# Gate columns of four tokens written interleaved into a PSUM bank, and copied out in runs of four

## The reference, cut to what matters

```python
def peer_tokens(xt, w_q, sub_keys, u_experts, v_experts):
    ...
    top_s, j = lax.top_k(cand, PEER_TOPK)
    e = (jnp.take_along_axis(i1, j // PEER_TOPK, axis=-1) * N_KEYS
         + jnp.take_along_axis(i2, j % PEER_TOPK, axis=-1))
    gate = jax.nn.softmax(top_s, axis=-1).astype(xt.dtype)
    u = jnp.take(u_experts, e, axis=0)
    v = jnp.take(v_experts, e, axis=0)
    act = jax.nn.gelu(jnp.einsum('td,thkd->thk', xt, u), approximate=False)
    return jnp.einsum('thk,thkd->td', gate * act, v)
```

## Time and profile before

| what | value |
|---|---|
| median of 3 runs | 1476.38 us (1474.99 to 1478.65) |
| span of the profiled execution | 1475.5 us, the one time that was recorded for it |
| TensorE busy, instructions | 98%, 8568 matmuls |
| VectorE, ScalarE, GpSimd busy | 84%, 43%, 60% |

### The profile page before, as it was taken

One profiled execution on the slowest core, in us unless ns is written; L12 is line 12 of the kernel. 1 busy time (PEld: TensorE's weight loads), 2 busy tenths in 40 slices (PEclk: granted clock), 3 DMA queues, 4 the chain that ended last, 5 costly groups with the idle time before them and its releaser, 6 DMA issues.

```text
span 1475.5 us, 24979 instructions
## 1 busy us (share of the span) xinstructions
PE 1448.1 (98%) x8568; PEld 1323.0 (90%) x8568; DVE 1240.7 (84%) x2516; ACT 628.3 (43%) x846; POOL 885.5 (60%) x552
## 2 busy tenths in 40 slices
PE   6998989999999999999999999999999999999998
PEld 6998989999999999999999999888888888888886
DVE  7999883799999999687888762799999999999985
ACT  6334544333333333366666653433333333333333
POOL 4687533648588888766667666355545555555510
PEclk9999999999999999999999999999999999999999
DMA  5222212748699999879999999999999999999972
GB/s 179 101 72 71 90 58 88 255 144 305 192 334 336 334 331 337 292 268 367 368 353 377 362 367 406 379 373 378 383 403 379 404 382 396 377 407 376 386 248 92
DMA packets 120259, 433.35 MB, mean 294 GB/s; under 512 B 12384, under 2 KB 12640, under 8 KB 118528
## 3 DMA queue, kind: packets, MB, share of 16 engines
q1 hardware_dynamic: 62592, 212.88, 40.0%
q0 software_dynamic: 46080, 167.79, 30.1%
q10 hardware_dynamic: 11520, 51.93, 8.8%
HBM read 379.34 MB, written 52.69 MB: 293 GB/s over the span
## 4 chain that ended last, share of the span: by engine, by line
PE 83%; DVE 1%; issue 0%; ACT 0%; DVEq 0%; ACTq 0%
PE ps_unit L848 36%; PE ps_misc L917 24%; PE ps_unit L917 12%; PE ps_unit L821 6%; PE ps_misc L883 3%; PE ps_misc L786 1%; PE ps_misc L790 0%; PE ps_unit L773 0%; PE ps_misc L913 0%; DVE gate_parts L1599 0%; DVE gate L1552 0%; PE ps_unit L913 0%; PE ps_misc L804 0%; PE ps_misc L902 0%; PE ps_misc L865 0%
## 5 line engine op out<-in xcount | busy, mean ns | idle before, releaser
L514 POOL TENSOR_TENSOR w_lo<-raw,w_hi 128x1024 fp32r<-128x1024 f32 x172 | 417.3, 2428 | 210.5 <-issue 127.6
L578 POOL DMA_INDIRECT rows<-v_rows,expert x160 | 258.8, 1617 | 234.7 <-DVE sums L1464 162.7
L963 ACT ACTIVATE w_hi<-raw 128x1024 fp32r<-128x1024 f32 x300 | 315.4, 1052 | 43.0 <-ACT act_ring L1138 33.7
L1454 DVE CUSTOM_DVE_ANT_0 rows<-rows,ps_unit 128x1024 f32<-128x1024 f32 x160 | 190.8, 1215 | 30.8 <-DMA rows<-u_rows,expert 30.5
L1182 ACT ACTIVATE prod_hi<-prod 128x384 fp32r<-128x384 f32 x128 | 67.3, 526 | 343.1 <-PE ps_unit L917 337.5
L848 PE MATMUL ps_unit<-mov_hi,w_hi 128*128 128x384 f32 x1024 | 205.3, 342 | 0.0
L848 PE MATMUL ps_unit<-mov_hi,w_lo 128*128 128x384 f32 x1024 | 199.9, 337 | 0.0
L848 PE MATMUL ps_unit<-mov_lo,w_hi 128*128 128x384 f32 x1024 | 199.8, 337 | 0.0
L848 PEld LDWEIGHTS ps_unit<-mov_lo,w_hi 128*128 128x128 f32 x1024 | 181.0, 188 | 0.0
L848 PEld LDWEIGHTS ps_unit<-mov_hi,w_lo 128*128 128x128 f32 x1024 | 180.9, 188 | 0.0
L848 PEld LDWEIGHTS ps_unit<-mov_hi,w_hi 128*128 128x128 f32 x1024 | 178.6, 189 | 0.2 <-issue 0.2
(11 more groups left out here) (257 smaller groups left out, 2570.1 us busy)
## 6 DMA issues: line engine op xcount, KB each, us to landing
raw<-stream SPq DMA_DIRECT2D x300, 512.0 KB, 6.0
acts_dram<-act_ring ACTq DMA_DIRECT2D x64, 384.0 KB, 6.4
gates_dram<-gates ACTq DMA_DIRECT2D x12, 2048.0 KB, 10.6
acts_in<-acts_dram SPq DMA_DIRECT2D x32, 768.0 KB, 8.3
gates_even<-gates_dram SPq DMA_DIRECT2D x12, 1024.0 KB, 13.2
gates_odd<-gates_dram SPq DMA_DIRECT2D x12, 1024.0 KB, 12.8
rows<-u_rows,expert POOLq DMA_INDIRECT x160, 7.0
rows<-v_rows,expert POOLq DMA_INDIRECT x160, 8.3
```

The costliest lines, as they stand in the source:

```text
L514: nc.gpsimd.tensor_tensor(w_lo[:, j, :], raw[:, j, :], w_hi[:, j, :].bitcast(F32), ALU.subtract).then_inc(lo_made, 1)
L578: nc.gpsimd.indirect_dma_start(out=rows[:, n % ROWS_RING, :], out_offset=None, in_=table, in_offset=bass.IndirectOffsetOnAxis(ap=expert[:, ...
L963: nc.scalar.activation(w_hi[:, j, :], raw[:, j, :], ACT.Copy).then_inc(hi_made, 1)
L1454: nc.vector.tensor_tensor_reduce(out=rows[:, n % ROWS_RING, :], in0=rows[:, n % ROWS_RING, :], in1=x_rows, scale=1.0, scalar=0.0, op0=ALU. ...
```

## The change

TensorE's output for token x is no longer 128 neighbouring columns but every fourth column of the bank, starting at x. ScalarE reads the bank with the four tokens of a key as neighbours and writes runs of four neighbouring fp32 (16 bytes), one run every 128 bytes. Operands, counts, waits, banks and the layout of `gates` are the same.

```diff
--- before.py
+++ after.py
@@ -880,7 +880,8 @@
                     pe.wait_ge(g_took, n - 1)
                 for x in range(BATCH):
                     for m, g in enumerate((gated_hi, gated_lo)):
-                        last = nc.tensor.matmul(ps_misc[:, b % 2, x * P:(x + 1) * P], hot_j[:, b % 2, x // 2, :, x % 2],
+                        last = nc.tensor.matmul(ps_misc[:, b % 2].rearrange("p (i t) -> p t i", t=BATCH)[:, x, :],
+                                                hot_j[:, b % 2, x // 2, :, x % 2],
                                                 g[:, b % 2, x // 2, :, x % 2], start=(m == 0), stop=(m == 1))
                 last.then_inc(g_done, 1)
 
@@ -1155,8 +1156,8 @@
                 u_unit(U_BEFORE - 1, j)
             def take_gates(tg, s, b):
                 act.wait_ge(g_done, BATCHES * tg + b + 1)
-                nc.scalar.activation(gates[:, s, :, BATCH * b:BATCH * (b + 1)].rearrange("p i t -> p t i"),
-                                     ps_misc[:, b % 2, :].rearrange("p (t i) -> p t i", t=BATCH),
+                nc.scalar.activation(gates[:, s, :, BATCH * b:BATCH * (b + 1)],
+                                     ps_misc[:, b % 2, :].rearrange("p (i t) -> p i t", t=BATCH),
                                      ACT.Copy, scale=1.0 / GATE_UP).then_inc(g_took, 1)
 
             def gate_group(tg):
```

## The result

The changed kernel takes 1512.12 us (median of 4 runs, 1510.94 to 1513.29), before it was 1476.01 us (median of 4, 1474.99 to 1478.65): a ratio of 1.0244 with a 95% interval of 1.0232 to 1.0256, 36.1 us slower. The forecast was 1515.6, with a likeliest range of 1506 to 1523.

What follows compares the result with a forecast made beforehand. TensorE was taken to bound the kernel. Span 1475.5 + 39.2 for scattered matmuls - 0 for shorter copies = 1514.7 us, plus 0.9 from span to median: 1515.6; likeliest range 1506 to 1523, 8 in 10 1473 to 1523.

Steps and rivals of the forecast that it cites:

- The bound: Gate groups, 626 to 872 us: TensorE busy 245.95 of 246.00 us, every other engine waits for it.
- The copy: ScalarE's 96 gate copies, line 1158: from 1167 to 650-750 ns each, saving up to 52.8 us, worth nothing at the end.
- The start of the value stage: After the gates: their last transfer starts about a microsecond earlier, but six microseconds of slack make that worth nothing.
- The price of a scattered matmul: TensorE's gate matmuls, line 883: from 57 to 108 ns each, by ScalarE's copy ratio 1167 / 617 = 1.89.
- A: Gate matmuls: PSUM takes scattered results as fast as neighbouring ones, still 57 ns, 1476 us; chance 0.30.
- B: Gate matmuls: each element pays ScalarE's full 1.07 ns, 106 us more, 1582 us; chance 0.06 with all else above the range.
- C: Gate matmuls: only each pair's accumulating one slows, 19.6 us, 1496 us; chance 0.05 with other prices between no change and forecast.
- The sum: TensorE's path in the gate groups: 768 gate matmuls at 51 ns more each, 39.2 us added, span 1514.7 us.
- D, faster: Gate groups: shorter ScalarE copies release something on the path, some 5 us through the value stage's start, 1471 us; chance 0.03.

Runs made afterwards that it cites:

- the step of 12 bytes: Kernel before, with three tokens' columns interleaved 12 bytes apart, the fourth token in one run, ScalarE copying in two instructions: 1503.39 us, against 1472.37.
- the first experiment: Kernel before with only ScalarE's copy changed to write runs of four, TensorE writing its columns as before: 1476.72 us against 1476.22, ratio 1.0004.
- TensorE's half alone: Kernel before with only the gate matmuls' output interleaved, ScalarE still writing single elements 128 bytes apart: 1513.15 us against 1476.22, ratio 1.0246.

## Why the prediction was right, point by point

**The bound.** That TensorE sets the beat and nobody else is on the path held: it stayed busy for 282.50 of 282.50 us, and the one half of the change that helps ScalarE moved nothing when run alone (ratio 1.0004).

**The copy.** The range of 617 to 1167 ns, with 650 to 750 as the choice, was too high, even at its lower bound: 590 ns. The row taken for that bound, line 1146, is a single copy of its form, and why it took longer stays open; the copies of line 1091, in the same trace, took 595 on average for the same 512 elements:

```profile
L1091 ACT ACTIVATE scores<-ps_misc 128x512 f32<-128x512 f32 x8 | 4.8, 595 | 0.0
L1091 ACT ACTIVATE scores<-ps_misc 128x256 f32<-128x256 f32 x8 | 3.1, 391 | 0.0
```

Nothing on ScalarE's side of the sum hung on it, but the price of the matmul did: by 595 the ratio is 1.96 in place of 1.89, a matmul 112 ns and the sum 42 us.

**The start of the value stage.** As forecast nothing came of the earlier transfer: VectorE's first product waits 15.84 us for the gates in the changed kernel (16.24 in the earlier trace rows), and the stage from the run of 240 matmuls on is 590.2 us (590.1).

**The price of a scattered matmul.** Taken as 108 ns by the ratio of two rows of ScalarE, measured as 109; the rivals A (57) and B (195) fall, and C (a slow second matmul only) with them, since the two of a token start at equal distances. What the runs show is an 8-byte place: pairs at even columns cost 57 ns, pairs at odd ones 109, steps of 8, 12 and 16 bytes 109 or 110. The Trainium skill's page "Advanced Engine Details and Errata", section "Memory Cachelines", gives PSUM lines of 8 bytes, two fp32 values. These figures agree with it. The same section says that any non-contiguous pattern slows matmuls significantly. The runs do not bear that out so widely: the pairs are not contiguous and cost nothing (ratio 0.9997). The ratio of ScalarE's rows gave the right number for a reason that the runs only half bear out. The prediction said that neighbours share an access and scattered elements don't; that fits what TensorE's matmuls cost. But its 1.89 is a property of ScalarE's writes to SBUF, with a fixed part in both durations. By an estimate from the two rows of line 1091, 391 ns for 256 elements and 595 for 512, that part is some 187 ns, and without it the ratio is 2.3 to 2.4. That the 1.89 came so near TensorE's 1.91 was luck.

**The sum.** 768 x 51 = 39.2 us was forecast, and the stretch lost 37.2. The term was too large by its count, not by its price: not all 16 matmuls of a beat pay the surcharge in the beat. The 14 distances from the second gate matmul to the sixteenth grow by 52 ns each, 0.73 us; the first distance grows only from 0.07 (703.74 to 703.81) to 0.09 us (702.04 to 702.13), and the one from the last gate matmul to the U unit from 0.02 to 0.06. The row of before that starts this beat is

```profile
703.74 0.23 PE L883 MATMUL ps_misc<-gated_hi,hot_j 128*128 128x128 f16 x1
```

That makes 0.79 in place of 16 x 51 = 0.82 us, against 0.78 in the chain. With a run at the end of each batch the whole surcharge shows (the step of 12 bytes), so what is missing here is lost where the U unit follows; how the U unit takes it up stays open. Of the 3.3 us by which the forecast span (1514.7) exceeds the measured one, 2.0 are this term. The other 1.3 are the earlier start of the gates, told above, less the 0.1 us behind the stretch, and belong to no part of the change.

**The rivals on the other side.** "D, faster" had 0.03 and fell with the first experiment. A, no change, had 0.30: it was the right thing to fear, because the kernel's trace had no row on it, and it turns out to describe the same edit with even pairs in place of single columns.

## What to carry to other kernels

Before an engine is relieved of a scattered write, look at who has slack: here the copy had 65 us of waiting behind it and the matmul none, so the same scatter was free on one side and cost 37 us on the other. If TensorE must interleave results in a PSUM bank, do it in pairs of fp32 columns that begin at an even one; that kept its pace here, single columns halved it at every step tried (8, 12 and 16 bytes). This is shown for fp16 matmuls of 128 columns alone. Here the reader of PSUM makes it needless: ScalarE read the bank at a step of 512 bytes for the same 590 ns.

## What the runs showed of the hardware that was not expected

ScalarE's reads from PSUM did not care for their order in these runs: written in runs of four, 512 elements took 591 ns in the median when read at 512 bytes apart (ScalarE's half alone), in address order (the changed kernel), or at 8 bytes apart (pairs). Its scattered writes took 1162 ns when reading at 16 bytes apart (TensorE's half alone) against 1164 in address order (the kernel before). What it pays for is single elements written 128 bytes apart; runs of two already cost nearly as little as runs of four. The source views of the copy in the kernel before, in the changed kernel, and with the step of 8 bytes, which writes runs of two:

```profile
L1158 ACT ACTIVATE gates<-ps_misc x96: 1110/1164/1227, 628.1 to 872.3; 128x512 f32<-128x512 f32 x96
L1159 ACT ACTIVATE gates<-ps_misc x96: 577/591/603, 626.6 to 906.9; 128x512 f32<-128x512 f32 x96
L1159 ACT ACTIVATE gates<-ps_misc x96: 627/644/662, 624.1 to 904.5; 128x512 f32<-128x512 f32 x96
```

And part of a scattered matmul's price is paid by the one behind it: a run that follows a scattered matmul has its own successor start after 0.09 us, not 0.06, while the first scattered matmul behind a run has its successor start after 0.07, not 0.11 (the step of 12 bytes).
